# A two-layer hybrid decoder step: value rounds given fixed places, and key and value rows of a second tile fetched alternately

## The reference

```python
q = (xt @ wq).reshape(PEER_BLOCK, PEER_HEADS, 2, PEER_HALF)
s = einsum('thpk,hpnk->thpn', q, subkeys)
s1, i1 = top_k(s[:, :, 0], 16);  s2, i2 = top_k(s[:, :, 1], 16)
cand = s1[..., :, None] + s2[..., None, :]
sc, pos = top_k(cand, 16)                       # 8 heads x 16 = 128 experts a token
gate = softmax(sc)
act  = gelu(einsum('thed,td->the', u[expert], xt))   # key rows, 1024 floats each
out  = einsum('the,thed->td', gate * act, v[expert]) # value rows, 1024 floats each
```

## Time and profile before

| | |
|---|---|
| median of 3 runs | 3005.95 us (3002.08 to 3012.62) |
| the profiled execution | 3016.86 us, span of its instructions 3015.1 us |
| TensorE, matmuls | 1900.0 us busy (63%) |
| VectorE | 1597.0 us (53%) |
| GpSimd | 1327.4 us (44%) |
| ScalarE | 275.6 us (9%) |
| mean granted TensorE clock | 0.794 of full speed |
| moved by DMA | 828.10 MB, 275 GB/s over the span |

### The profile page before, as it was taken

One profiled execution on the slowest core, in us unless ns is written; L12 is line 12 of the kernel. 1 busy time (PEld: TensorE's weight loads), 2 busy tenths in 40 slices (PEclk: granted clock), 3 DMA queues, 4 the chain that ended last, 5 costly groups with the idle time before them and its releaser, 6 DMA issues.

```text
span 3015.1 us, 26084 instructions
## 1 busy us (share of the span) xinstructions
PE 1900.0 (63%) x9857; PEld 1191.7 (40%) x9857; DVE 1597.0 (53%) x2984; ACT 275.6 (9%) x434; POOL 1327.4 (44%) x1160
## 2 busy tenths in 40 slices
PE   5879857838858776657687676777454785003533
PEld 2469523327836335444264236453232372000100
DVE  4253386575844526867312336865765256884033
ACT  1111010010110010010100101011110000000000
POOL 0000012443623555645322444466764225887774
PEclk8889978967879887777798787888677897555875
DMA  7430586964768997767999888698989657899997
GB/s 269 168 128 1 203 293 218 345 216 133 231 218 287 325 339 251 251 214 237 335 340 326 301 284 310 237 353 322 325 306 360 240 187 288 302 326 384 409 409 315
DMA packets 296712, 828.10 MB, mean 275 GB/s; under 512 B 45951, under 2 KB 57135, under 8 KB 296589
## 3 DMA queue, kind: packets, MB, share of 16 engines
q0 software_dynamic: 165888, 604.05, 55.3%
q1 hardware_dynamic: 120132, 218.02, 20.6%
q10 hardware_dynamic: 10568, 4.38, 0.6%
HBM read 816.05 MB, written 10.31 MB: 274 GB/s over the span
## 4 chain that ended last, share of the span: by engine, by line
PE 33%; DVE 21%; DMA 20%; POOL 14%; issue 7%; ACT 3%; PEld 1%; SPq 0%; ACTq 0%; DVEq 0%; PEldq 0%; POOLq 0%
PE psum L1908 31%; POOL arena L709 9%; DVE arena L1096 6%; DMA arena<-in_peer_v,idx_v 6%; DVE arena L1113 6%; POOL wring L709 5%; DMA wring<-in_ada_w 2%; DMA wring<-in_gla_w_in 2%; DMA wring<-in_rw_w_rkv 2%; DMA out<-arena 2%; DMA wring<-in_peer_wq 2%; PE psum L1926 1%; DMA vring<-mod_d 1%; ACT arena L755 1%; DVE hT L1096 1%
## 5 line engine op out<-in xcount | busy, mean ns | idle before, releaser
L709 POOL DMA_INDIRECT arena<-in_peer_u,idx_u x476 | 631.1, 1326 | 952.1 <-DVEq L1692 411.0
L1908 PE MATMUL psum<-arena 128*32 128x512 f32 (+7 forms) x3666 | 615.5, 574 | 400.8 <-DMA arena<-in_peer_v,idx_v 163.8
L1113 DVE CUSTOM_DVE_ANT_0 arena<-arena,hc 128x1024 f32<-128x1024 f32 x476 | 565.2, 1224 | 261.8 <-DMA arena<-in_peer_u,idx_u 221.3
L709 POOL DMA_INDIRECT arena<-in_peer_v,idx_v x428 | 433.4, 1013 | 604.5 <-PE psum L1908 444.0
L1908 PEld LDWEIGHTS psum<-arena 128*32 128x32 f32 (+2 forms) x3666 | 318.1, 170 | 624.9 <-issue 477.5
L1908 PE MATMUL psum<-pick,ident 128*128 128x256 f32 x1046 | 268.4, 412 | 48.6 <-DVEq L1364 40.0
L1908 PE MATMUL psum<-wring,arena 128*32 128x512 f32 (+3 forms) x808 | 230.1, 693 | 85.5 <-DMA wring<-in_peer_v,idx_v 42.3
L1908 PEld LDWEIGHTS psum<-pick,ident 128*128 128x128 f32 x1046 | 211.1, 208 | 138.5 <-issue 58.9
L1908 PE MATMUL psum<-wring,hT 128*128 128x512 f32 (+1 forms) x480 | 185.2, 544 | 12.5 <-DMA wring<-in_gla_w_in 10.3
L1908 PE MATMUL psum<-hT,wring 128*128 128x128 f32 (+3 forms) x1312 | 178.1, 299 | 13.7 <-DMA wring<-in_peer_wq 4.0
L1908 PEld LDWEIGHTS psum<-hT,wring 128*128 128x128 f32 (+1 forms) x1312 | 167.0, 199 | 35.1 <-issue 19.6
(11 more groups left out here) (224 smaller groups left out, 1819.2 us busy)
## 6 DMA issues: line engine op xcount, KB each, us to landing
wring<-in_ada_w SPq DMA_DIRECT2D x24, 2048.0 KB
wring<-in_peer_wq SPq DMA_DIRECT2D x20, 2048.0 KB
wring<-in_rw_w_rkv SPq DMA_DIRECT2D x12, 2048.0 KB
wring<-in_gla_w_in SPq DMA_DIRECT2D x12, 2048.0 KB
wring<-in_rw_wo SPq DMA_DIRECT2D x6, 2048.0 KB
vring<-mod_d SPq DMA_DIRECT2D x22, 512.0 KB
wring<-in_gla_wo SPq DMA_DIRECT2D x4, 2048.0 KB
arena<-in_peer_u,idx_u POOLq DMA_INDIRECT x476, 6.1
```

The costliest lines, as they stand in the source:

```text
L709: pool.indirect_dma_start(slot(s, n), None, v_rows if side else u_rows, bass.IndirectOffsetOnAxis(index, 0)).then_inc(rows_landed[s], 16)
L1113: dve.tensor_tensor_reduce(slot(s, n), slot(s, n), hc[:, t, :], 1.0, 0.0, MUL, ADD, acts[:, (3 * li + t) % 2, col:col + 1]).then_inc(rows_ ...
L1908: return nc.tensor.matmul(out, lhsT, rhs, start=start, stop=stop)
```

## The change

`MINGLED` gets layer 1, tile 1: the second half of its key rounds takes turns with the first half of its value rounds. For that, TensorE's tail opens 16 value rounds after the first half of the weights and 16 after the second, and VectorE's tail sets `weigh` and `build` ahead of `last_norm(0)`. A helper, `rounds_now(n)`, does n value rounds at once, if so many are left. It is called for 3 rounds in `core(1)`; for 1 round after the output product in layer 0's `out` of tile 1 and of sample (layer 1 keeps its 4); and, where sample is among the tiles, after each of the four query blocks: 1 round in layer 0, 2 in layer 1.

```diff
-MINGLED = ((1, 0),)
+MINGLED = ((1, 0), (1, 1))
...
 ScalarE, tail
-            gelu(1, 1, 0)
+            weights_due(1, 1, 0)
             root(rstd[:, 0, 0:1])
-            deal_weights(1, 1, 0)
...
 VectorE, tail
             open_rows(1, 1, 0, 72, 0)
-            rest_rows(8)
+            rest_rows(6)
+            weigh(1, 1, 0)
+            rest_rows(3)
+            build(1, 1, 0)
+            rest_rows()
             last_norm(0)
-            rest_rows(4)
-            weigh(1, 1, 0)
-            rest_rows()
-            build(1, 1, 0)
...
 TensorE
+            def rounds_now(n):
+                for _ in range(min(n, stream.left)):
+                    stream.left -= 1
                     value_round()
...
                 for _ in END_MODS[t]:
                     modulation()
+                if t == 1:
+                    rounds_now(3)
                 operands()
                 turn(y, for_scalar()).then_inc(psum_for_scalar, 1)
...
                 for b in held:
                     release(b, psum_for_vector, nfv[0])
-                for _ in range(min(stream.left, 4) if li and tiles[0] else 0):
-                    stream.left -= 1
-                    value_round()
+                if tiles[0]:
+                    rounds_now(4 if li else 1)
...
                         last.then_inc(psum_for_scalar, 1)
                         asked = nfa[0]
+                        if SAMPLE in tiles:
+                            rounds_now(2 if li else 1)
...
             fan_weights(1, 1, 0)
+            open_values(1, 1, 0, 16)
+            rest_values(0)
             fan_weights(1, 1, 1)
-            open_values(1, 1, 0)
+            open_values(1, 1, 0, 16, 16)
             rest_values(0)
```

More of the change, by code:

```diff
@@ L1856, in serve @@
                 for _ in range(stream.due(work, product)):
+                    value_round()
+            def rounds_now(n):
+                for _ in range(min(n, stream.left)):
+                    stream.left -= 1
                     value_round()
```

## The result

After the change the kernel takes 2980.97 us, the median of 5 runs (2977.84 to 2986.71); the kernel before took 3012.62 beside it (5 runs, 3002.08 to 3017.33). The ratio is 0.9907, its 95% interval 0.9882 to 0.9932: 28 us faster by the ratio (20 to 36), where 55 were forecast. The ratio is worked out from all runs of both kernels and need not equal the quotient of the two medians. The profiled execution took 2977.84 us, with a span of 2976.0.

The account below looks back on a forecast made before the run. VectorE's waits in the VectorE-TensorE chain were taken as the bound up to 2561 us, then GpSimd's gather queue. -26.4 - 10.6 - 4.5 - 13.6 = -55.1 gave a median of 2950.8 us, range 2928 to 2985 (about 0.82).

Parts of the forecast that it names:

- B: Sample, layer 0: 1 round after the output product and each query block; 12 us lost, 22.6 given back, -10.6 us.
- C: Layer 1: 2 rounds after each query block; second scores 13.2 us later, 17.7 won at the spread indices, -4.5 us.
- the dealt rounds cost what they give: Rival: B ends at +1.4 and C at +8 because both wait on gathers, giving 2975 us; chance 0.2.
- A: Layer 0: 3 rounds in `core(1)` and 1 in tile 1's `out` shorten VectorE's wait for tile 0's sum, -26.4 us.
- the stream is four rounds ahead: Step of A: four rounds done early, nearly free, make tile 0's sum ready near 1103.7 in place of 1130.
- the term of 12 us: Step of B: waits for rows and late weights bring TensorE to the GLA's first block 12 us later.
- the return of 22.6: Step of B: at the end of the GLA `add_experts` starts at 1759.7 in place of 1782.3, -22.6 us.
- bound of 24: Upper bound on B's delay before the GLA: twice the forecast's own 12 us, with the DMA at 0.88 share.
- the two further pairs lie under its `choose`: Step of C: after the second block of scores VectorE is the bound, so the last two pairs of rounds are hidden.
- The return, 17.7: Step of C: VectorE's wait of 19.90 us before the spread indices shrinks to about 2.2.
- D: Layer 1's mingled tile 1: 128 gathers beside 64 products at 1.33 us each, last landing 2 us sooner; -13.6 us.
- Rival one: Each product costs GpSimd a fixed price wherever it stands, so D gives nothing: 2964 us, chance 0.15.

Follow-up runs that it names:

- slim pair: `slim_before` and `slim_dealt`: query weights cut to 8 of 512 columns, without and with B's rounds; sample's stage 60.3 and 85.9 us.
- `only_queries`: Kernel before with only the 2 value rounds after each query block of layer 1's last `out`: 3012.53 us, ratio 1.0022.
- `late_rounds`: Changed kernel without B and C, but in layer 1 with 2 rounds behind the first query block, 3 behind the second block's scores: 2964.28 us, ratio 0.9857.
- `slim_before`: Kernel before with query-weight blocks (sample in layer 0, tile 1 and sample in layer 1) loading 8 of 512 columns; sample's stage 60.3 us, one execution.
- `slim_dealt`: `slim_before` plus the rounds of B, and those of C in layer 1; sample's stage in layer 0 85.9 us, one execution.

## Why the prediction was right or wrong

The direction was right and the time lies inside the range, but the size is half the forecast: -28 in place of -55. That the time is inside is owed to the width of the range and not to the sum: two of the four terms, B and C, have the wrong sign by the traces. Of the rivals, "the dealt rounds cost what they give" came nearest (2975), and its mechanism is the one found; it was still too mild, since B and C don't break even, they lose.

**A was right.** The wait before tile 0's sum fell to 5.21 us, predicted 5.8, and the wait of 26.67 us was filled. The term -26.4 is -27.0 by the traces at that place. Its cost was put at 0.4 and is some 5: the argument that the stream is four rounds ahead and therefore nothing waits left out that the slots are then empty, and that the next served round stands in front of the scores. Timed -24.

**B is the step that failed**, and in it the term of 12 us; the return of 22.6 was right (21.0 by the traces). The prediction counted 12 x 6.6 = 79 us of slot time against the 74 of the stage, walked through it to a wait of 6.6 us at the third block, and came to 12 us; the traces give 30.7. Both numbers for the pace were borrowed: 6.6 us a round from tile 0's stage, and landing at 6.1 us from the tail. In this stage landing is 9.2, in the trace of before already. Put into the prediction's own walk, with two groups of slots, this gives as an estimate (5.0 + 8.3 + 1.9 to 3.64) / 2 = 7.6 to 8.5 us a round, or 91 to 102 us for twelve: 19 to 30 more than the stage's 72. Afterwards the stage measures 101.8 and 101.9, which is 8.5 a round. The transfers say the same beforehand. The windows view of the kernel before, for this very stretch (columns as in the earlier trace rows):

```profile
1510.00:1590.00 80.00, 64.34 (x474) 48.94 (x473) 17.27 (x37) 5.61 (x10) 26.30 (x28) 0.92 0.93 346
```

Five rounds are 20 x 0.524 = 10.5 MB, and at 346 GB/s that is 30 us, in a stage whose DMA is already 0.93 busy. The prediction read the share from a window of 342 us, 0.88 at 318 GB/s, and used it only as a reason for its bound of 24. The slim pair keeps this from being the whole story: there the DMA share over the stage is 0.78 without B's rounds and 0.90 with them, and the five rounds still cost 25.6. The limit of the slots and that of the transfers lie close together here, and how the price is shared between them is not settled.

**C failed by a miscount and by the same waits.** The second block of scores comes 22 us later in place of 13.2. VectorE's first block came 12 us later, near the 10 expected. Then the prediction let "the two further pairs lie under its `choose`", but by the order of the code only the fourth pair does: the third stands ahead of the second block's scores, as the lines of `only_queries` above show, and it costs 8 to 12 us where 3 were left. The return, 17.7 by the wait of 19.90, is 16.4, since that wait is 15.0 to 20.5 us in the other kernels without C: a single profile had it near the top. `late_rounds`, with two rounds ahead of these scores in place of six, shows that nearly all of the return can be had for 4 us.

**D was right in its mechanism.** 1.318 us a gather, no wait of GpSimd for a value round, 10 us in place of 13.6. The price that a product has for GpSimd isn't fixed: (1.318 - 1.25) x 128 = 8.7 us over 64 products, 0.14 each, as in the lighter of the two stretches of the earlier trace rows (0.16) and far from 0.48. Rival one, no gain at all, is thus refuted: 0.9965 with 0.9987 as its upper end. The Trainium skill (SBUF — State Buffer, "SBUF: two separate sides") calls the port pair shared by VectorE and GpSimd an exclusive lock, held for a whole instruction, and the prediction made of it the rival of a fixed price for each product. The runs refute the fixed price (0.48, 0.16 and 0.14 us); whether such a lock is behind what GpSimd loses isn't tested here.

The 3.6 us that D is short can be traced in part. The sum "170 against 181" leaves 11 and not 11.6, and with the unrounded 1.57 and 1.25 only 10. The same 128 gathers, from the 17th key round on, take 183.1 us in the kernel before, the longest of the eight kernels without D (176.0 to 183.1, mean 178.9), and 167.2 to 169.0 with D (mean 168.1): a gain of 10.8 us. And the last gather lands 0.7 us sooner, by the means from its issue to 3003.07, where 2 were forecast.

Together: A 2 short of its term, B 22, C 12, D 3, some 39 by the timed parts; the whole change came out 27 short.

## What to carry to other kernels

Price a piece of work that is moved into a stage by the pace and the landing time of *that* stage, read from its own rows in a narrow window, and count pieces times pace against the stage's length: below it they are nearly free, near it they begin to cost, and above it each costs most of its pace (3.4 us from five to seven rounds, 6.0 from seven to twelve, here). When a transfer comes with each piece, its bytes over the stage's own rate are a second count, made in one line. Put such work behind what the next engine waits for and not in front of it: six more rounds ahead of the scores cost 22 us, two ahead and three behind cost 4. Count in the code's order which pieces stand ahead of what is awaited. A wait read from one profile is good to some us; when a term is a wait's whole length, expect the mean of several to be smaller.

## What the runs showed of the hardware

- A gather of 512 KB landed 6.1 us after its issue (median) beside key products and 13.9 us when value gathers followed each other back to back, both with no loads of weights beside it; 9.2 (up to 13.6) while the weights' loads of 2 MB ran beside it; 7.9 and 6.6 with these loads cut to 8 columns (`slim_before`, `slim_dealt`).
- Transfers of rows of 4 KB held 399 to 408 GB/s for 245 us in the tail of the kernel after, at a DMA share of 1.02 to 1.03; in the query stage slices of 2.5 us reach the same, and the mean of 351 is brought down by twelve slices of 28 to 356.
- What VectorE's products cost GpSimd went with whether VectorE paused: by estimates from gathers per stretch, 0.48 us a product without pause (one stretch of 30 us), 0.16 and 0.14 with pauses. No run changes the pauses alone.
